# Ahead of the last mixer of a 1-core Trainium2 kernel: later constants, norm pieces of two tiles, rotation by transfers, later side steps

## The chip, the cores and the metric

One Trainium2 chip, one of its NeuronCores. The engines are named as the profile names them: PE (TensorE), DVE (VectorE), ACT (ScalarE), POOL (GpSimd) and SP (SyncE, which here only issues transfers). The metric is the device time of one execution in microseconds, and the median of several.

## What is computed

256 tokens with 2048 features pass through two blocks of two layers each. The first block:

```python
cos, sin = rope_tables(positions)
for layer in range(DEPTH):                       # DEPTH = 2
    if layer < N_A_LAYERS:
        mix = short_conv_mixer(x, a_w_in[layer], a_conv_w[layer], a_w_out[layer])
    else:
        k_sh, v_sh = shared_kv(x, kv_w_k, kv_w_v, cos, sin)
        mix = diff_attention(x, k_sh, v_sh, cos, sin, b_w_q[j], b_lambda[j],
                             b_subln_g[j], b_w_o[j], lambda_init)
    x = layer_norm(DEEPNORM_ALPHA * x + mix, ln_g[layer, 0], ln_b[layer, 0])
    ffn = conv_ffn(x, ffn_w_up[layer], ffn_conv_w[layer], ffn_conv_b[layer], ffn_w_down[layer])
    x = layer_norm(DEEPNORM_ALPHA * x + ffn, ln_g[layer, 1], ln_b[layer, 1])
```

The second block runs, on rmsnorm(h), a layer AB (dilated attention with three strides beside chunked gated linear attention, GLA), then a layer CD (an S5 state space mixer beside an HGRN mixer), each added to h, and ends with an rmsnorm:

```python
h = h + ab_layer(rmsnorm(h, norm_g[0]), ab_w_in, gla_w_gate, gla_b_gate, gla_norm_g, ab_w_out)
h = h + cd_layer(rmsnorm(h, norm_g[1]), cd_w_in, ..., hgrn_norm_g, cd_w_out)
return rmsnorm(h, final_g)
```

Two pieces of it are touched by name. The rotation of keys and queries works on the first 32 of each head's 128 features:

```python
x1, x2 = rot[..., :half], rot[..., half:]        # half = 16
rotated = concatenate([x1 * c - x2 * s, x2 * c + x1 * s], axis=-1)
```

and the attention's lambda is exp(sum(lam0·lam1)) − exp(sum(lam2·lam3)) + lambda_init.

## The kernel before

**Tiling.** Features lie on the partitions: XA[128, 16, 256] holds the residual stream in fp32 as 16 tiles of 128 features by 256 tokens, XH and XL the high and low bf16 halves of the activation that feeds the next product. A weight matrix is cut into chunks of 512 rows by 512 columns. Each product of fp32 numbers is three bf16 products (high·high, high·low, low·high), so that a chunk is 4 tiles × 4 column blocks × 3 = 48 matmuls of 128x256, about 5.2 us of PE.

**The road of a chunk.** SP loads it (1 MB) into the ring WF, three deep (L467). ACT casts it to the high half WH (L1169), DVE subtracts for the low half WL (L1746), both in a ring of five, up to LA = 3 chunks ahead of PE. PE multiplies in `gemm` (L652 on; all matmuls are recorded at L645, in the helper `mm`). The last KEPT = 46 chunks take another road: POOL loads them early in two pieces of 512 KB (L543), splits them (L552, L557) and stores both halves to DRAM (L554, L559), and SP loads halves at the end of the program (L460). `keep_begin(n)` says after which chunk of PE piece n is split.

**What sets the order.** Each engine runs a program of its own, written in the order in which it issues; nothing is scheduled. Work beside the products ("side flows") is written as generators, and a step of them (the code up to the next `yield`) is taken `rate` times per chunk: on PE after the second tile of a chunk and at its end, on ACT and DVE in one batch behind the split of the chunk three ahead. `idle(n)` is n empty steps. So one `yield` more puts the rest of a side flow later on that engine, by half a chunk of PE at rate 3. Engines wait in order: an instruction that waits holds up all behind it.

**Stages on PE** (us of the trace): short-conv mixer 0 to 251, its output product to 360, norm 0, feed-forward 364 to 1072, norm 1, keys and queries in eight groups of four chunks 1077 to 1262, values to 1375, output product to 1460, norm 2, feed-forward 1482 to 2183, norm 3, layer AB 2190 to 2640, layer CD 2640 to 3128, last rmsnorm to 3143.

**Places the change touches.**

- The start of SP's program: the order of the first loads (L474 to L490). CN are constants (identity, the rotation matrix `rope`, masks), PR the parameters, POSI the token positions.
- The layer norm: the norm is taken in pieces of the 16 tiles, EAGER = (first tile, tiles). DVE subtracts the mean (L1875) and multiplies by 1/sigma (L1894); ACT applies gain and bias in place (L1264 and L1270 for the first two tiles, L1275), copies the high half (L1279; at norm 3 it multiplies by the rmsnorm's gain, L1285); DVE makes the low half (L1859, at norm 3 L1854). PE takes the tiles in order as they become ready (the `ready` branch, L698 to L709).
- `attention_tables` and `lambda_sums`: angles and sines of the rotation on DVE and ACT, and lambda: two products on DVE (L2043, L2044), a column sum on PE, an exponential on ACT.
- The rotation: PE multiplies the first 32 rows of a key or query group by the 32x32 matrix `rope`, which swaps the two halves of 16 rows and changes a sign (the function `rotate`, four fp32 records each); DVE multiplies this by the sines (L2070), the rows themselves by the cosines (L2071), and adds (L2073).
- `diff_scores`, `heads`, `outputs`: scores, exponentials, the transposition ("turn"), products with the values and the norm of each head (L1328, L1331 on ACT, L2122, L2125 on DVE; OF is the tile of one head's output).
- Layer AB: `rms_sums`, `gla_decay` (DVE scan ahead of L1746), and the dilated heads: scores, softmax over three strides (L2300, L2301 on DVE end it), turn (L857 to L859 on PE), product.
- The end: DVE multiplies three groups of four tiles (L2531), POOL one (L636), SP stores four groups (L496).

Of the kernel before, what the change touches and what calls it, by code (L numbers as in the profile page):

```python
# [12 lines left out]
ALU = mybir.AluOpType  # L13
# [4 lines left out]
T = 256  # L18
# [9 lines left out]
FIRST = 4  # L28
KEPT = 46
# [17 lines left out]
CONST, NCONST = columns([("ident", 128), ("rope", 32), ("freq", 1), ("eps5", 1), ("eps6", 1), ("one", 1),  # L47
# [8 lines left out]
def constants():  # L56
# [7 lines left out]
    rope = np.zeros((128, 32))  # L64
    for i in range(16):
        rope[i + 16, i] = -1.0
        rope[i, i + 16] = 1.0
    put("rope", rope)
# [129 lines left out]
def two_block_model(nc, A, out):  # L198
    ctx = ExitStack()
    with ctx:  # L200
# [3 lines left out]
        def sem(name):  # L204
# [17 lines left out]
        ROOT = sb("ROOT", [128, 5])  # L222
        PSG = [ctx.enter_context(nc.psum_tensor(f"PSG{i}", [128, 4, T], F32)) for i in range(2)]
# [3 lines left out]
        d_in, d_pos, d_s5c, d_gw, d_cwst, d_csst, d_cwld = (  # L227
            sem(n) for n in ("d_in", "d_pos", "d_s5c", "d_gw", "d_cwst", "d_csst", "d_cwld"))
# [9 lines left out]
        d_out = [sem(f"d_out{i}") for i in range(2)]  # L238
# [15 lines left out]
        s_msq, s_var, s_sqrt, s_nrm, s_pre = (sem(n) for n in ("s_msq", "s_var", "s_sqrt", "s_nrm", "s_pre"))  # L254

        s_ang, s_trig, s_lamp, s_lams, s_lame = (sem(n) for n in ("s_ang", "s_trig", "s_lamp", "s_lams", "s_lame"))
        s_rot, s_rope, s_score, s_ss, s_max, s_exp, s_aa, s_tr, s_at = (
            sem(n) for n in ("s_rot", "s_rope", "s_score", "s_ss", "s_max", "s_exp", "s_aa", "s_tr", "s_at"))
# [15 lines left out]
        s_xw, s_rr, s_store, s_store_g = sem("s_xw"), sem("s_rr"), sem("s_store"), sem("s_store_g")  # L274
# [45 lines left out]

        def bcl(ap, n):
            return ap.unsqueeze(2).broadcast_to([ap.shape[0], ap.shape[1], n])
# [29 lines left out]
        EAGER = [(0, 1), (1, 1), (2, 2), (4, 4), (8, 4), (12, 4)]  # L352
# [45 lines left out]
        ATT = dict(SS=scr(13824, 2, 384), PP=scr(14592, 2, 384), SM=ASM, OF=scr(18816, 2, T), OQ=scr(19328, 2, T))  # L398
# [57 lines left out]
        def sync_program():  # L456
# [32 lines left out]
            for i in range(FIRST + 2, first_kept):  # L489
                load(i)  # L490
# [4 lines left out]
            def store(g, done_out):  # L495
                nc.sync.dma_start(out_v[:, 4 * g:4 * g + 4, :], four(XW, g)).then_inc(done_out, 16)  # L496
# [2102 lines left out]
```

## Time and profile before

| | |
|---|---|
| median of 3 runs | 3145.56 us |
| all runs | 3145.50, 3145.56, 3147.03 us |
| profiled execution | 3144.75 us |
| its span | 3143.4 us |
| mean granted clock of PE | 0.992 |
| PE busy | 3047.8 us (97%) |
| DVE, ACT, POOL busy | 2167.4 (69%), 1465.1 (47%), 680.8 us (22%) |
| data moved | 693 MB, mean 221 GB/s |

The profiled execution took 1.35 us more than its span, the time around the first and the last instruction. Matmul records overlap their neighbours, so that one row of 0.27 us stands for some 0.11 us of PE's time. The busy shares are those of the whole; the sections below go by stretches. A row of a timeline gives start, duration, engine, line, operation, what is written and read, how many in a row, and in brackets the idle time ahead of it with what ended it. The column "clock" of the windows is the share of PE's full clock that was granted: 1.00 is 2.4 GHz, 0.50 is 1.2 GHz.

### The profile page before, as it was taken

The numbers are of one execution on the slowest core, as the hardware profiler recorded it, in microseconds if no ns is written. First come the engines' busy times: TensorE is split into PE (matmuls) and PEld (weight loads), VectorE is DVE, ScalarE is ACT, GpSimd is POOL, SyncE is SP. The second block draws the span as 40 slices with busy tenths as digits, with TensorE's granted clock in tenths as the row PEclk, the third lists the DMA queues.
The fourth block names the chain that finished last, engine by engine and source line by source line (L and its number), as shares of the span: only waits on it lengthen the run. The fifth ranks groups of instructions, "written<-read, shape, count | busy, mean of one in ns | idle before, by whom it ended". The sixth has DMA issues, their size and how long they took to land. (4 is left out here: it accounts for less than half of the span.)

```text
span 3143.4 us, 58119 instructions
## 1 busy us (share of the span) xinstructions
PE 3047.8 (97%) x26006; PEld 2593.7 (83%) x26006; DVE 2167.4 (69%) x2028; ACT 1465.1 (47%) x1418; POOL 680.8 (22%) x753
## 2 busy tenths in 40 slices
PE   8999899999999999999999999999999999999988
PEld 7888788888888888568888888888687878776877
DVE  6777777777757666556767877655776556896655
ACT  4333454545444444564555555434564444212543
POOL 3555144545455200000210000000130000012300
PEclk9999999999999999999999999999999999999999
DMA  9889488888898564544666656754455545554343
GB/s 334 284 311 320 161 283 306 297 299 306 303 325 284 191 206 162 174 159 150 233 230 223 231 206 218 262 201 137 160 175 178 175 172 189 200 211 177 133 150 108
DMA packets 306025, 693.29 MB, mean 221 GB/s; under 512 B 16480, under 2 KB 20704, under 8 KB 299760
## 3 DMA queue, kind: packets, MB, share of 16 engines
q1 hardware_dynamic: 270192, 564.22, 52.1%
q0 software_dynamic: 35584, 125.36, 11.0%
q8 instruction: 204, 3.34, 0.4%
q14 instruction: 45, 0.37, 0.0%
HBM read 625.56 MB, written 63.96 MB: 219 GB/s over the span
## 5 line engine op out<-in xcount | busy, mean ns | idle before, releaser
L645 PE MATMUL PSG<-XH,WS 128*128 128x256 bf16 x11296 | 1846.5, 274 | 24.9 <-DVE WS L1963 7.4
L1746 DVE TENSOR_TENSOR WS<-WF,WS 128x2048 bf16<-128x2048 f32 (+1 forms) x483 | 1190.3, 2486 | 590.9 <-ACT WS L1169 590.3
L645 PE MATMUL PSG<-XL,WS 128*128 128x256 bf16 x5648 | 1490.4, 274 | 1.8 <-DVE XL L1854 1.1
L645 PEld LDWEIGHTS PSG<-XH,WS 128*128 128x128 bf16 x11296 | 1107.6, 98 | 173.6 <-issue 27.2
L1169 ACT ACTIVATE WS<-WF 128x2048 bf16<-128x2048 f32 (+1 forms) x483 | 906.0, 1899 | 632.7 <-PE PSG L645 216.9
L645 PE MATMUL PSG<-SCR,WS 128*128 128x256 bf16 x6720 | 745.5, 273 | 3.6 <-DVE SCR L2315 3.6
L645 PEld LDWEIGHTS PSG<-SCR,WS 128*128 128x128 bf16 x6720 | 659.5, 98 | 86.2 <-issue 4.2
L645 PEld LDWEIGHTS PSG<-XL,WS 128*128 128x128 bf16 x5648 | 554.0, 98 | 71.9 <-DVE XL L1859 2.4
L557 POOL TENSOR_TENSOR SCR<-SCR 128x1024 bf16<-128x1024 f32 x92 | 239.9, 2607 | 5.6 <-DMA weight_halves<-SCR 4.0
L645 PE MATMUL PSG<-WS,XH 128*128 128x512 bf16 x640 | 190.1, 379 | 2.2 <-issue 2.2
L645 PE MATMUL PB<-SCR 128*128 128x128 f32 (+3 forms) x928 | 151.2, 326 | 24.2 <-issue 7.8
L645 PEld LDWEIGHTS PB<-SCR 128*128 128x128 f32 (+2 forms) x928 | 126.4, 191 | 44.5 <-issue 24.6
L2018 DVE SCALAR_TENSOR_TENSOR SCR<-PSG,PR,SCR 128x254 f32<-128x254 f32 (+1 forms) x352 | 142.4, 471 | 17.7 <-ACT SCR L1398 17.1
L543 POOL DMA_DIRECT2D SCR<-cd_w_in x80 | 58.0, 725 | 415.8 <-PE PSG L645 401.1
L645 PEld LDWEIGHTS PSG<-WS,XH 128*128 128x128 bf16 x640 | 62.6, 98 | 76.7 <-issue 4.8
L1398 ACT ACTIVATE SCR<-PSG,PR 128x256 f32<-128x256 f32 x176 | 84.8, 562 | 69.4 <-PE PSG L645 69.3
L645 PE MATMUL PSG<-WS,XL 128*128 128x512 bf16 x320 | 116.1, 379 | 0.0
L552 POOL CAST SCR<-SCR 128x1024 bf16<-128x1024 f32 x92 | 110.6, 1203 | 3.5 <-PE PSG L645 3.4
L571 POOL DMA_DIRECT2D SCR<-s_cT_re x1 | 0.5, 542 | 437.8 <-DVE XL L1859 437.8
L1190 ACT ACTIVATE SCR<-PSG 128x1024 f32<-128x1024 f32 x30 | 30.6, 1020 | 133.1 <-PE PSG L645 133.1
L587 POOL DMA_DIRECT2D s_rotation<-SCR x16 | 8.5, 532 | 381.3 <-ACT SCR L1500 381.3
L525 POOL TENSOR_TENSOR SCR<-SCR 128x128 f32<-128x128 f32 x84 | 40.4, 482 | 174.0 <-PE PB L645 112.9
(267 smaller groups left out, 1779.7 us busy)
## 6 DMA issues: line engine op xcount, KB each, us to landing
WF<-ffn_w_up SPq DMA_DIRECT2D x176, 1024.0 KB, 6.5
WF<-ffn_w_down SPq DMA_DIRECT2D x88, 1024.0 KB, 6.4
WF<-ab_w_in SPq DMA_DIRECT2D x56, 1024.0 KB, 5.2
weight_halves<-SCR POOLq DMA_DIRECT2D x184, 256.0 KB, 6.0
WS<-weight_halves SPq DMA_DIRECT2D x46, 1024.0 KB, 4.8
WF<-a_w_in SPq DMA_DIRECT2D x44, 1024.0 KB, 8.9
SCR<-cd_w_in POOLq DMA_DIRECT2D x80, 512.0 KB, 6.9
WF<-a_w_out SPq DMA_DIRECT2D x16, 1024.0 KB, 8.0
```

The lines of the kernel that those rows point to most:

```text
L525: nc.gpsimd.tensor_tensor(to[:, :, 0:half], mid, src[:, :, 0:half], ALU.subtract)
L543: nc.gpsimd.dma_start(KW[n % 2], src).then_inc(d_keep[n % 2], 16)
L552: t = own.mark(nc.gpsimd.tensor_copy(KH, w))
L557: t = own.mark(nc.gpsimd.tensor_tensor(KL, w, KH, ALU.subtract))
L571: nc.gpsimd.dma_start(CT[i].rearrange("p a b -> p (a b)"), A[name]).then_inc(d_s5c, 16)
L587: nc.gpsimd.dma_start(CSD[n], TCS).then_inc(d_csst, 16)
L645: return nc.tensor.matmul(o, lhsT, rhs, start=start, stop=stop, skip_group_check=True)
L1169: act(shaped(WH, i % RB, rows, g["width"]), shaped(WF, r % RF, rows, g["width"]), ACT.Copy).then_inc(s_hi, 1)
L1190: act(dst, rowwise(ps) if row_major else ps[:, :, :], func, scale=scale).then_inc(s_evac[gi % 2], 1)
L1398: t = act(dst[:, n, :], ps[:, n, :], ACT.Identity, bias=pr("f_bias", 88 * l + f), scale=pr("f_conv", 264 * l + 176 + f))
L1746: tt(l, w, h, ALU.subtract).then_inc(s_lo, 1)
L2018: ins = stt(dst[:, n, sh:T], ps[:, n, 0:T - sh], pr("f_conv", 264 * l + 88 * tap + f), dst[:, n, sh:T], ALU.mult, ALU.add)
```

## The change

1. **Start.** CN and the positions are loaded behind the 32nd chunk, CN with a semaphore of its own; POOL's early pieces begin at chunk 10 and 12 of PE rather than 2 and 4, in the same total time; two chunks fewer are split early (KEPT 44).
2. **Norm.** EAGER has (4, 2), (6, 2) in place of (4, 4). For pieces of one or two tiles, and for all of norm 3, ACT makes the high half straight from XA with gain and bias as its scale and offset, and brings XA itself up to date after that. For norm 3 the gains are products made in advance (GWB). DVE's order is written anew (`multiply`, `whole`, `low`).
3. **PE within a piece:** the products with XH of all its tiles come first, then those with XL (`held`).
4. **Rotation.** The swap of the two halves of 16 rows is made by two DMAs of POOL (64 KB each) into the tile RT; the sign goes into the frequencies; PE's matmuls for it are gone. DVE waits for the DMAs (`d_swap`), PE's scores for the rotation (`s_rope`).
5. **Side steps.** `lambda_sums`, `diff_scores`, `heads`, `rms_sums`, `gla_decay` and the dilated heads have more empty steps; a second OF tile.
6. **End.** DVE multiplies all four groups, the last one in two halves; five stores instead of four.

The core of the diff:

```diff
-KEPT = 46
+KEPT = 44
+CONSTANTS_AT = 32
...
-    col[0:16, 0] = freq
+    col[0:16, 0] = -freq
     col[16:32, 0] = freq
...
-        EAGER = [(0, 1), (1, 1), (2, 2), (4, 4), (8, 4), (12, 4)]
+        EAGER = [(0, 1), (1, 1), (2, 2), (4, 2), (6, 2), (8, 4), (12, 4)]
...
-            nc.sync.dma_start(CN[:, :], A["consts"]).then_inc(d_in, 16)
             nc.sync.dma_start(PR[:, :], A["params"]).then_inc(d_in, 16)
+            for i in range(FIRST + 2, CONSTANTS_AT):
+                load(i)
+            nc.sync.dma_start(CN[:, :], A["consts"]).then_inc(d_cn, 16)
             nc.sync.dma_start(POSI, A["positions"].partition_broadcast(128)).then_inc(d_pos, 16)
...
-                return 4 + 2 * n if n < 28 else 67 + 2 * (n - 28)
+                return 12 + 2 * n if n < 24 else 67 + 2 * (n - 24)
...
-            nc.gpsimd.wait_ge(s_mm, 2)
+            nc.gpsimd.wait_ge(s_mm, 10)
...
+            for j in range(4):
+                for r, t in ((0, KA[j % 2]), (1, QA[j % 2])):
+                    nc.gpsimd.wait_ge(*evac(stage["kq"][2 * j + r]))
+                    if j or r:
+                        nc.gpsimd.wait_ge(s_rope, 2 * j + r)
+                    nc.gpsimd.dma_start(RT[16:32, :, :], t[0:16, :, :]).then_inc(d_swap, 16)
+                    nc.gpsimd.dma_start(RT[0:16, :, :], t[16:32, :, :]).then_inc(d_swap, 16)
...
-            nc.gpsimd.tensor_tensor(four(XW, 1), four(XW, 1), bc(STAT[:, 3, :], 4), ALU.mult).then_inc(s_store_g, 1)
...
-                            if ready[k] != seen:
-                                seen = ready[k]
-                                nc.tensor.wait_ge(*seen)
-                            for o, first, ab in sums:
-                                last = mm(o, *ab[1], False, sp)
+                            held += [(o, ab[1], sp) for o, _, ab in sums]
+                            if i < FIRST or kk == nk - 1 or ready[k + 1] != ready[k]:
+                                if ready[k] != seen:
+                                    seen = ready[k]
+                                    nc.tensor.wait_ge(*seen)
+                                for o, ab, stop in held:
+                                    last = mm(o, *ab, False, stop)
+                                held = []
...
             def lambda_sums():
-                yield
-                yield
-                yield
+                yield from idle(7)
                 nc.tensor.wait_ge(s_lamp, 1)
...
             def diff_scores(h, q, k, first):
+                nc.tensor.wait_ge(s_rope, 2 * (h // 2) + 2)
                 yield from scores(h, q, k, (first, first + 1))
-                yield
-                yield
+                yield from idle(3)
                 yield from turn(h, AA, (s_aa, h + 1))
...
-            def heads(j, gen):
-                yield from gen
-                yield
+            def heads(j):
+                yield from idle(4)
...
                     yield from scores(8 + h // 2, QD0, KD0, (h, h + 1))
+                    yield
                     yield
                     for c in range(2):
                         yield
...
                 for p, (a, n) in enumerate(EAGER):
                     nc.scalar.wait_ge(s_nrm, PIECES * L + p + 1)
+                    if L == 3 or n < 4:
+                        for k in range(a, a + n):
+                            w, b = high_affine(L, k)
+                            t = act(XH[:, k, :], XA[:, k, :], ACT.Identity, bias=b, scale=w)
+                        t.then_inc(s_xh, 1)
+                        if p >= 2:
+                            affine(a, n).then_inc(s_aff, 1)
+                        if p == 4:
+                            nc.scalar.wait_ge(s_pre, 2 * L + 2)
+                            nc.scalar.wait_ge(a_own, own.mark(affine(0, 2)))
                     else:
-                        weighted_high(0, a, n)
+                        affine(a, n).then_inc(s_aff, 1)
+                        nc.scalar.wait_ge(s_aff, (PIECES - 2) * L + p - 1)
+                        act(XH[:, a:a + n, :], XA[:, a:a + n, :], ACT.Copy).then_inc(s_xh, 1)
...
+                    OF = ATT["OF"][h % 2]
+                    yield from head_norm(h, 2, "eps5", OF, ATT["OQ"], h + 1, (s_nlo, h - 1) if h >= 2 else None)
...
             def rotate(n, dst):
                 yield
-                nc.vector.wait_ge(s_rot, n + 1)
+                yield
+                nc.vector.wait_ge(d_swap, 32 * (n + 1))
                 nc.vector.wait_ge(s_trig, 1)
...
-                tt(RT[0:32, :, :], sw, b32(SIN), ALU.mult)
+                tt(RT[0:32, :, :], RT[0:32, :, :], b32(SIN), ALU.mult)
...
                 t.then_inc(s_gabs, 1)
+                yield
+                yield
                 nc.vector.wait_ge(s_lg, 1)
...
-            for g in (0, 2, 3):
+            for g in range(4):
                 nc.vector.wait_ge(s_xw, g + 1)
-                tt(four(XW, g), four(XW, g), bc(rr, 4), ALU.mult).then_inc(s_store, 1)
+                for h in range(2 if g == 3 else 1):
+                    x = XW[:, 14:16, :] if h else XW[:, 12:14, :] if g == 3 else four(XW, g)
+                    tt(x, x, bc(rr, 2 if g == 3 else 4), ALU.mult).then_inc(s_store, 1)
```

How the instructions stand at three places (xN: a row repeated; in brackets the semaphores waited for).

**SP at the start, before.** WF is the weight ring, XA the input tiles.

```order
L472 DMA WF<-a_w_in 128x512 [waits s_lo0] x4
L467 DMA WF<-a_w_in 128x4x512 [waits s_lo0] x2
L486 DMA CN<-consts 128x2598
L487 DMA PR<-params 128x1082
L488 DMA SCR<-positions 128x256
L467 DMA WF<-a_w_in 128x4x512 [waits s_lo0]
L467 DMA WF<-a_w_in 128x4x512 [waits s_lo] x41
L467 DMA WF<-a_w_out 128x4x512 [waits s_lo] x16
```

Now:

```order
L475 DMA WF<-a_w_in 128x512 [waits s_lo0] x4
L470 DMA WF<-a_w_in 128x4x512 [waits s_lo0] x2
L489 DMA PR<-params 128x1082
L470 DMA WF<-a_w_in 128x4x512 [waits s_lo0]
L470 DMA WF<-a_w_in 128x4x512 [waits s_lo] x25
L492 DMA CN<-consts 128x2566
L493 DMA SCR<-positions 128x256
L470 DMA WF<-a_w_in 128x4x512 [waits s_lo] x16
```

CN and the positions stand behind 26 more chunk loads; the parameters stay.

**ACT at norm 0, before.** XH is the high half, XA the stream.

```order
L1264 ACTIVATE XH<-XA,PR 128x256 [waits s_nrm] x2
L1270 ACTIVATE XA<-XA,PR 128x256 [waits s_pre]
L1270 ACTIVATE XA<-XA,PR 128x256
L1275 ACTIVATE XA<-XA,PR 128x256 [waits s_nrm,a_own]
L1275 ACTIVATE XA<-XA,PR 128x256
L1279 ACTIVATE XH<-XA 128x512 [waits a_own]
L1275 ACTIVATE XA<-XA,PR 128x256 [waits s_nrm]
L1275 ACTIVATE XA<-XA,PR 128x256 x3
L1279 ACTIVATE XH<-XA 128x1024 [waits a_own]
L1275 ACTIVATE XA<-XA,PR 128x256 [waits s_nrm]
```

Now:

```order
L1261 ACTIVATE XH<-XA,PR 128x256 [waits s_nrm] x3
L1261 ACTIVATE XH<-XA,PR 128x256
L1252 ACTIVATE XA<-XA,PR 128x256 x2
L1261 ACTIVATE XH<-XA,PR 128x256 [waits s_nrm]
L1261 ACTIVATE XH<-XA,PR 128x256
L1252 ACTIVATE XA<-XA,PR 128x256 x2
L1261 ACTIVATE XH<-XA,PR 128x256 [waits s_nrm]
L1261 ACTIVATE XH<-XA,PR 128x256
L1252 ACTIVATE XA<-XA,PR 128x256 x2
L1252 ACTIVATE XA<-XA,PR 128x256 [waits s_pre]
L1252 ACTIVATE XA<-XA,PR 128x256
L1252 ACTIVATE XA<-XA,PR 128x256 [waits s_nrm,a_own]
```

The high halves of six tiles more are direct, ahead of the update of XA; tiles 4 to 7 are no longer one copy.

**PE at the first rotation, before.** PSG is the bank of the running product, PB the side bank, SCR the key tile, CN the constants.

```order
L645 MATMUL PSG<-XH,WS 128x256 x2
L645 MATMUL PSG<-XL,WS 128x256
L645 MATMUL PSG<-XH,WS 128x256
L645 MATMUL PB<-SCR,CN 32x512 [waits s_evac0]
L645 MATMUL PB<-SCR,CN 32x512
L645 MATMUL PSG<-XH,WS 128x256
L645 MATMUL PSG<-XL,WS 128x256
```

**POOL there, now.** SCR is both RT and the key and query tiles.

```order
L550 DMA weight_halves<-SCR 128x1024 [waits g_own]
L553 TENSOR_TENSOR SCR<-SCR 128x1024 [waits d_kl]
L555 DMA weight_halves<-SCR 128x1024 [waits g_own]
L570 DMA SCR<-SCR 16x1024 [waits s_evac0]
L571 DMA SCR<-SCR 16x1024
L570 DMA SCR<-SCR 16x1024 [waits s_rope,s_evac1]
L571 DMA SCR<-SCR 16x1024
```

PE's rows with CN at the rotation are gone; POOL's transfers, two for each of the eight groups, follow its last early split.

## Rows read from the trace of the kernel before

**Rows 1.** Page, part 1: busy time, share and instructions of PE.

```profile
PE 3047.8 (97%) x26006; PEld 2593.7 (83%) x26006; DVE 2167.4 (69%) x2028; ACT 1465.1 (47%) x1418; POOL 680.8 (22%) x753
```

**Rows 2.** PE's waits over the span: who waited, for whom, total us, times, longest.

```profile
PE PSG L645 <- ACT XH L1279: 6.8, 6, 1.5
...
PE PSG L645 <- DVE WS L1746: 5.5, 3, 4.3
...
PE PB L857 <- DVE SCR L2301: 5.4, 3, 3.3
PE PB L645 <- DVE SCR L2044: 5.2, 1, 5.2
PE PB L645 <- ACT SCR L1331: 4.8, 2, 3.2
...
PE PSG L645 <- issue: 2.2, 1, 2.2
PE PSG L645 <- ACT XH L1285: 2.1, 3, 1.2
...
PE PSG L645 <- DVE XL L1854: 1.1, 2, 0.6
```

**Rows 3.** Windows around 395 us: us, PE busy (records), clock, DMA share, GB/s.

```profile
394.10:397.50 3.40, 3.27 (x16) 0.50 0.67 197
397.50:402.50 5.00, 5.00 (x48) 1.00 0.83 286
```

**Rows 4.** Timeline, ACT, 38 to 41 us: start, us, operation, idle before it, releaser.

```profile
39.36 1.91 ACT L1169 ACTIVATE WS<-WF 128x2048 bf16<-128x2048 f32 x1 [8.26 <-DMA WF<-a_w_in]
```

**Rows 5.** Windows at the start, columns as in rows 3.

```profile
40.00:45.00 5.00, 0.71 (x7) 0.75 1.03 383
45.00:50.00 5.00, 5.00 (x28) 0.57 0.84 283
```

**Rows 6.** DMA issues: queue, count, KB each, median us from issue to landing.

```profile
CN<-consts SPq DMA_DIRECT2D x1, 1299.0 KB, 11.3
...
SCR<-s_bT_im POOLq DMA_DIRECT2D x8, 64.0 KB, 3.0
...
SCR<-positions SPq DMA_DIRECT2D x1, 128.0 KB, 12.1
```

**Rows 7.** Norm 0: timeline of ACT; line L1279 (ns min/median/max); timelines of PE, DVE.

```profile
376.25 2.08 ACT L1275 ACTIVATE XA<-XA,PR 128x256 f32<-128x256 f32 x4 [0.63 <-DVE XA L1894]
...
L1279 ACT ACTIVATE XH<-XA x12: 629/1057/1057, 368.2 to 1496.2; 128x1024 bf16<-128x1024 f32 x9, 128x512 bf16<-128x512 f32 x3
...
383.60 1.05 PE L645 MATMUL PSG<-XH,WS 128*128 128x256 bf16 x8
...
381.25 4.49 DVE L1746 TENSOR_TENSOR WS<-WF,WS 128x2048 bf16<-128x2048 f32 x2 [0.58 <-ACT WS L1169]
```

**Rows 8.** Rotation: PE by form over the span; then ACT, DVE, PE near 1130 us.

```profile
L645 PE MATMUL PB<-SCR,CN 32*32 32x512 f32 x32 | 15.2, 593 | 0.0
...
1125.14 1.02 ACT L1190 ACTIVATE SCR<-PSG 128x1024 f32<-128x1024 f32 x1 [8.02 <-PE PSG L645]
...
1130.20 1.21 DVE L2070 TENSOR_TENSOR SCR<-PB,SCR 32x1024 f32<-32x1024 f32 x1
...
1134.74 1.47 PE L645 MATMUL PB<-SCR 128*128 128x256 f32 x8
```

**Rows 9.** POOL's store issues at L554: duration ns min/median/max, first, last.

```profile
L554 POOL DMA_DIRECT2D weight_halves<-SCR x92: 540/557/575, 32.4 to 1055.2; - x92
```

**Rows 10.** Window at the first rotation, columns as in rows 3.

```profile
1100.00:1110.00 10.00, 10.00 (x80) 1.00 0.99 333
```

**Rows 11.** Timeline, ACT, 1390 to 1395 us.

```profile
1392.59 0.60 ACT L1328 ACTIVATE SCR<-PB 128x512 f32<-128x512 f32 x1 [0.82 <-DVE SCR L2125]
```

**Rows 12.** The end: line L2531 on DVE, and a window (DVE busy).

```profile
L2531 DVE TENSOR_TENSOR SCR<-SCR,STAT x3: 1210/1226/3362, 3132.8 to 3137.3; 128x1024 f32<-128x1024 f32 x3
...
3138.00:3143.40 5.40, 0.47 (x1) 0.50 0.85 291
```

More of the change, by code:

```diff
@@ L237, in two_block_model @@
         d_kh, d_kl = sem("d_kh"), sem("d_kl")
-        d_out = [sem(f"d_out{i}") for i in range(2)]
+        d_out = sem("d_out")
+        d_swap = sem("d_swap")
         d_bt = [sem(f"d_bt{i}") for i in range(2)]
@@ L913, in tensor_program @@
                     side.until(pairs[j - 2])
-                side.add(rotate(2 * j, KA[j % 2], gk))
+                side.add(idle(3))
                 gemm(gq, xh, xl, rate=3)
-                pairs.append(side.add(heads(j, rotate(2 * j + 1, QA[j % 2], gq))))
+                pairs.append(side.add(heads(j)))
             for j, gi in enumerate(stage["v"]):
@@ L924, in rms_sums @@
             def rms_sums():
-                yield from idle(7)
+                yield from idle(8)
                 sum_features(24, 1, True, False)
@@ L1304, in rms_first @@
                         yield
-                yield from idle(7)
+                yield from idle(9)
                 nc.scalar.wait_ge(s_sumrd, 28)
                 rms_root(0)
-                yield from idle(6)
+                yield from idle(4)
                 for p in range(4):
@@ L1420, in attention_tables @@
                 act(COS, TRT[:, 2, :], ACT.Sin, bias=cn("halfpi"), scale=-1.0).then_inc(s_trig, 1)
-                yield
-                yield
+                yield from idle(6)
                 nc.scalar.wait_ge(s_lams, 1)
@@ L1436, in diff_scores @@
                 exps(h, ATT["SS"], ATT["PP"], ASM)
-                yield
-                yield
-                yield
+                yield from idle(4)
                 nc.scalar.wait_ge(s_tr, h + 1)
@@ L1444, in heads @@
             def heads(j):
-                yield from idle(3)
+                yield from idle(4)
                 yield from diff_scores(2 * j)
@@ L1931, in rms_first @@
                         yield
-                yield from idle(8)
+                yield from idle(9)
                 rms_factor(0)
-                yield from idle(5)
+                yield from idle(4)
                 for p in range(4):
@@ L2044, in attention_tables @@
                 tt(ASM[:, 37:38], lb[:, 2:3], lb[:, 3:4], ALU.mult).then_inc(s_lamp, 1)
-                yield
-                yield
+                yield from idle(8)
                 nc.vector.wait_ge(s_lame, 1)
@@ L2107, in diff_scores @@
                 t.then_inc(s_aa, 1)
-                yield from idle(4)
+                yield from idle(5)
             def heads(j):
```

139 lines of the change are left out of this document (58 added, 81 removed).

## The prediction

> **What bounds the kernel now.** I read the page's busy shares first, then the list of what TensorE (PE) waited for, then the stretches around each wait. PE is busy for 3047.8 of 3143.4 us [rows 1], so a step shortens the program only if PE issues less in it, waits less, or runs at its full clock instead of half. The list of PE's waits [rows 2] gives the places that the diff touches: 5.5 us on DVE's weight halves (three waits, one of 4.3), 6.8 us in six waits on L1279 (the layer norms), 5.2 us in one wait on L2044 (lambda), 4.8 us in two waits on L1331 (the head norm; 3.2, and so 1.6), 5.4 us in three waits on L2301 (the dilated heads; the longest 3.3), 2.2 us in one "issue" gap, and 2.1 and 1.1 us in small ones at the fourth norm (L1285, L1854). A full stretch holds 48 matmuls in 5.00 us, about a chunk. A stretch of 3.40 us behind the lambda wait ran at 0.50 of the clock [rows 3]: it lost 1.7 us. I look for such a stretch behind each long wait, because it goes with the wait.
>
> **Start: −6.6.** ACT's split of a chunk at 39.36 us had waited 8.26 us for the weight transfer [rows 4]; PE, who gets the halves after ACT and DVE, stood 4.3 us [rows 2]. The windows show the transfer engines at 1.03 of their share, and then PE at 28 matmuls instead of 48 in 5 us, clock 0.57 [rows 5]: 20/48 of 5 us, with the bit ahead of 45 us 2.3 us. In this queue stand CN (1299 KB) and the positions, 11.3 and 12.1 us from issue to landing [rows 6], and POOL's early pieces beside them. What had to be moved ahead of that chunk's end is the chunk (1.05 MB), CN (1.33), the parameters (0.55), the positions (0.13) and POOL's two pieces (1.05), 4.1 MB; the change leaves 1.6. At the 383 GB/s of [rows 5] that is 6.5 us less; the chunk lands near 33.4 us (I take 6 us), its two splits (1.9 and 2.3 us) end near 37.7, ahead of 40.4, where PE asked. So 4.3 + 2.3. Low end 2, if other transfers fill the space. At the new place of the moved loads PE has hardly a wait on halves (1.2 us of [rows 2] in the rest of the program): 0. If that cover is gone it is CN's 1.3 MB at 383 GB/s, 3.4 us.
>
> **Lambda: −6.8.** PE waits 5.2 us for two tiny DVE products, which stand behind a table computation and a weight half. Four more steps on PE are two chunks at this rate, some 10 us, well behind the 5.2. The half-clock stretch of [rows 3] starts with this wait: 5.2 + 1.6. Low end 5.2, if the clock falls anyhow. What is late next are the halves, which stay in their order on DVE.
>
> **Norms 0 to 2: +1.8.** Here I don't take the 6.8 us as a gain. At the fourth chunk PE resumed at 383.60, when the halves that DVE began at 381.25 were done (two in 4.49, the first 2.29 long) [rows 7]: PE was bound there by the halves, which stand on ACT behind its whole norm chain, and what it had waited before was hidden in that. So ACT's chain decides. It gains six direct operations of 0.52 (four take 2.08) and loses two copies (0.63 and 1.06) [rows 7]: +1.4 us, of which its idle time (0.63 in [rows 7], two shorter ones ahead) takes a part. I take +0.6 for each of three norms; between 0 and +1.4 each. In the list one wait of some 2 us on DVE's halves takes the place of the second one on L1279.
>
> **Rotation: −15.2.** 32 records of the 32x512 fp32 matmul are 15.2 us of PE time [rows 8], with PE full around them. This goes for sure; what may come back is a wait for the swaps. POOL issues two DMAs of 64 KB, 0.56 us each, as L554 [rows 9]; 64 KB landed in 3.0 us [rows 6]. In the second group ACT's copy of the bank ran from 1125.14 to 1126.16, so the swap is in at 1126.2+0.6+0.6+3.0 = 1130.4; DVE's rotation, three operations of 1.21 us, began at 1130.20 before and so ended near 1133.8, and PE's scores came at 1134.74 [rows 8]; the program puts them now two chunks (10.5 us) behind the group's end, 1135.6. Margin 1.8. Price 0; between 0 and the late swaps below. The first swap falls where the transfer engines are at 0.99 [rows 10].
>
> **Attention outputs: −4.1.** Both waits on L1331 are for an ACT copy behind DVE's L2125, for which ACT stood 0.82 us [rows 11], since there was one OF tile. With two tiles and a step more the wait of 1.6 goes; of the 3.2 the 0.8 goes, and then it is under 3 us, so that I take off its half-clock stretch too, 1.7. (The 2.2 us gap had none behind it.) Ends: −2.4 and −6.5.
>
> **Norm 3: −0.7.** Its small waits (2.1 and 1.1) vanish with a half-clock stretch of 1.7, but PE then waits for the sums of the next norm, which DVE makes behind ACT's chain; these 4.9 us come back there, and +1.4 with them, since ACT's chain is that much longer. The issue gap of 2.2 us was DVE in gla_decay with the next half queued behind it; two more yields put the half first: −2.1. Ends −3 and +4, the upper one if the merged wait (7 to 8 us) is followed by twice that half-clock stretch.
>
> **Dilated heads: −5.2.** Of the three waits on L2301 the longest is 3.3, the others 0.8 and 1.3. A yield more moves each turn half a chunk (2.6 us): 0.8 gone, 3.3 to 0.7 with its half-clock stretch (1.7), 1.3 gone, but the last pair's turn and product now meet ahead of the output projection: +1.2. −0.8−2.6−1.7−1.3+1.2. Ends −2 and −7.
>
> **End: −2.0.** The middle DVE multiply took 3.36 us beside POOL's, the others 1.21 and 1.23 [rows 12]. Four at 1.22, the last in two halves of 0.69, end near 3137.9. The three stores behind the first moved for 0.85 of the last 5.4 us [rows 12], 1.53 us each; back to back, from 3134.7 (an estimate: 0.6 behind the first multiply), all four take 6.1 us and end near 3140.8; with the 0.3 us that I leave to the span's end, −2.3, less a fifth store's overhead. −0.7 to −2.4.
>
> KEPT 46 to 44 puts two more splits on ACT and DVE near 3015 to 3026, where PE waits for other things: 0, at most +2. The rest of the S5 and HGRN part stays.
>
> **Sum.** −6.6−6.8+1.8−15.2−4.1−0.7−5.2−2.0 = −38.8. The profiled execution took 3144.75 (span 3143.4), so 3105.95; the median of the runs shown is 0.8 us higher, so 3106.8, say 3107.
>
> **A rule that speaks against it.** 92 issues from POOL beside a busy DVE took 540 to 575 ns, and POOL's 64 KB loads landed in 3.0 us [rows 6, 9]: nothing held them. The Trainium skill, "SBUF — State Buffer", section "SBUF: two separate sides", says that GpSimd itself writes the descriptors of the DMAs it issues, and that it is shut out from that while DVE runs an operation in a two-port mode; it advises SP's or ACT's queue. By that rule the swaps would be late wherever DVE runs such an operation; the sum would stay −38.8 if that is never the case, and come to rival 1 if it is once or twice.
>
> **Rivals.** (1) One or two swaps land late, as the positions did under full transfer engines, 12.1 us [rows 6]. The rope is then 12.1−3.0−2.0 = 7.1 us too late for PE, with up to 3.4 us of half clock: +10.5, 3117. For: 0.99 in the first stretch [rows 10]. Against: it lasts 10 us, and the first scores come a group later. 0.12. (2) The norms: the merged chain costs 1.4 at each of three, norm 3 comes to +4, and gaps near 3 us draw half-clock stretches of 1.7 at three: (4.2−1.8)+4.7+5.1 = +12, 3119. For: PE then meets all its waits in one place. Against: the 2.2 us gap. 0.13. (3) The change doesn't do what it says at the start, since POOL's pieces and the weights still fill the queue: +4.6 to +6.6, 3113. 0.07. (4) The slower side: swaps queue behind the 1 MB weight loads in all four pairs. One late swap costs 10.5; four cost 42, and 4.6 more if the second transfer waits behind the first (its issue twice): 3107+42 = 3149, or 3154. It decides from a landing of about 12 us on; the 3.0 of [rows 6] is against it, the 12.1 for it. 0.03 for 3149, 0.03 for 3154.
>
> **How the numbers follow.** My forecast has 0.62 (3100 to 3112), the rivals 0.12, 0.13, 0.07 and 0.06. 0.2% (6.3 us) is about what a measurement of this kernel can tell from no change. Faster by more: 0.62+0.12+0.13+0.07 = 0.94; within 0.2%: 0.03; slower: 0.03. The range: the low ends (norms 0, outputs −6.5, norm 3 −3, dilated −7, end −2.4, the others as they stand) give −47.5, 3098; the high end takes in rivals 1 to 3, 3121.
>
> **What would show it.** PE's busy time falls by some 20 (15.2, and the half-clock stretches, four or five fewer) and its idle time by some 17. No wait of PE at 40 us, none at 389; at the fourth chunk of norms 0 to 2 a wait on DVE's halves near 2 us; no wait of PE's scores on the DVE rotation; five stores without a pause. It is wrong if swaps land after more than 5 us, or if waits of 3 us and more appear where small ones stood.

## The result, and the profile after

The changed kernel took 3114.08 us in the median of four runs (3113.43 to 3115.98), against 3146.30 us for the kernel before on the same chip (four runs, 3145.50 to 3147.96). The ratio is 0.9898, with an interval of 0.9887 to 0.9910: 32 us faster, forecast 39 (3107, range 3098 to 3121). The profiled execution of the changed kernel is the slowest of its four: 3115.98 us, span 3114.7, so the two profiles stand only 28.7 us apart, and the account by stages below adds up to that, but for rounding.

The page's busy shares after the change, to be held against [rows 1]:

```profile
PE 3028.3 (97%) x25950; PEld 2592.8 (83%) x25974; DVE 2163.2 (69%) x2047; ACT 1474.2 (47%) x1432; POOL 666.5 (21%) x748
```

PE is busy for 19.5 us less: 15.2 of it are the matmuls that are gone. The rest is not the clock. Ahead of the end, the trace before has nine stretches at half clock, 40.8 us in all, with PE busy for 35.0 of them; the trace after has eight, 44.2 us, with PE busy for 35.0 again. (24 matmul records of the values' product are missing from the trace after, 25950 beside 25974 weight loads; what else makes up the rest is open.) With 28.7 us less of span PE's idle time falls by only 9. Its list of waits (who waited for whom, total us, times, longest), to be held against [rows 2]:

```profile
PE PB L645 <- DVE SUMS L1756: 10.4, 6, 6.4
PE PSG L645 <- DVE WS L1736: 9.4, 7, 2.1
...
PE PSG L645 <- DVE XL L2320: 4.8, 1, 4.8
PE PSG L645 <- ACT XH L1271: 3.9, 3, 1.3
...
PE PB L645 <- ACT SCR L1322: 2.3, 1, 2.3
PE PB L645 <- ACT SCR L1180: 1.5, 1, 1.5
...
PE PB L847 <- DVE SCR L2306: 1.0, 1, 1.0
```

The wait on lambda's products (5.2) is gone, that on the dilated turn fell from 5.4 to 1.0, the head norm's from 4.8 to 2.3, the "issue" gap of 2.2 is gone. Others grew: the weight halves from 5.5 to 9.4 (now L1736, seven times, none longer than 2.2), the wait for the sums to 10.4 with one of 6.4 that was not there, and the last one of the dilated stage (L2320, 2.9 before) to 4.8.

By stage (all numbers us, negative where the changed kernel is faster):

| stage | forecast | measured |
|---|---|---|
| start, to the first norm's sums | −6.6 | −5.6 |
| lambda | −6.8 | −3.1 |
| norms 0 to 2 | +1.8 | −0.1 |
| rotation | −15.2 | −15.5 |
| attention outputs | −4.1 | −2.3 |
| norm 3 and gla_decay | −0.7 | +1.2 |
| dilated heads | −5.2 | −2.6 |
| S5 and HGRN | 0 | +0.9 |
| end | −2.0 | −1.7 |
| sum | −38.8 | −28.8 |

The first row and the last four are read off from one of PE's waits to the next in both traces. The rows from lambda to the attention outputs lie between PE's resuming behind the first norm's sums and its resuming behind the head norm's wait (338.48 to 1393.73 us before, 332.88 to 1367.16 after), 21.0 us less. They are split by PE's weight loads for the main products: there are 24,624 of them in every trace here, in the same order, so that the time between the same two loads can be compared. From the load that stands at 386 us before to the one at 420 us (lambda and the first chunks of the feed-forward), PE took 34.0 us before and 31.0 after.

**Start.** The windows of the start (us, PE busy and records, clock, transfer share, GB/s), for [rows 5]:

```profile
30.00:35.00 5.00, 4.24 (x40) 1.00 0.67 217
35.00:40.00 5.00, 5.00 (x49) 1.00 0.88 297
40.00:45.00 5.00, 5.00 (x49) 1.00 0.79 262
```

No wait and no half clock at 40 us (one wait of 0.76 us stands at 30.9), and the transfer engines no longer at 1.03. In the twelve profiled runs below, which all keep both loads late or one of them, PE reached the first norm's sums at 329.2 to 330.6 us, and here at 331.1 (336.6 before), so the −5.6 of this trace is −6.0 to −7.4 in the others.

**Norm 0** has now a wait for the high halves and then the one on the weight halves (DVE) that the prediction looked for, 1.69 us. **Rotation.** DVE's operation with its wait, and the landing times of POOL's two transfers of each swap (min, median, max):

```profile
1100.39 1.21 DVE L2071 TENSOR_TENSOR SCR<-SCR 32x1024 f32<-32x1024 f32 x1 [0.41 <-DMA SCR<-SCR]
...
DMA to landing us min/median/max: 2.1/2.5/4.2
...
DMA to landing us min/median/max: 2.2/3.5/4.3
```

The longest swap took 4.3 us; DVE waited 2.9 us for four of the eight, PE for none.

**Norm 3.** ACT's last pieces and first weight split, PE's wait for the sums, and the window that holds its end and the half clock behind it. This one wait stands where [rows 2] had the small ones on L1285 and L1854:

```profile
2178.08 2.06 ACT L1252 ACTIVATE XA<-XA,PR 128x256 f32<-128x256 f32 x4
2180.17 1.91 ACT L1159 ACTIVATE WS<-WF 128x2048 bf16<-128x2048 f32 x1
...
2186.26 1.22 PE L645 MATMUL PB<-SUMS,ONE_D 128*128 128x256 f32 x2 [6.37 <-DVE SUMS L1756]
...
2183.10:2193.30 10.20, 6.43 (x24) 0.50 0.33 104
```

**End.** Five multiplies in 4.70 us, the stores back to back at 0.93, for [rows 12]:

```profile
3105.84 4.70 DVE L2538 TENSOR_TENSOR SCR<-SCR,STAT 128x1024 f32<-128x1024 f32 x5
...
3105.00:3108.00 3.00, 0.00 (x0) 0.50 0.00 0
3108.00:3114.70 6.70, 0.00 (x0) 0.50 0.93 313
```

### The profile page after: what moved, and what is told of

Same layout as the page of the kernel before. It is cut to its first block and busy times, and to the rows that moved or that the text cites. A ratio compares the mean times of both kernels' runs of the same rounds, so it can differ in the third digit from the quotient of the medians.

```text
span 3114.7 us, 58088 instructions
## 1 busy us (share of the span) xinstructions
PE 3028.3 (97%) x25950; PEld 2592.8 (83%) x25974; DVE 2163.2 (69%) x2047; ACT 1474.2 (47%) x1432; POOL 666.5 (21%) x748
## 5 line engine op out<-in xcount | busy, mean ns | idle before, releaser
L1736 DVE TENSOR_TENSOR WS<-WF,WS 128x2048 bf16<-128x2048 f32 (+1 forms) x485 | 1189.3, 2475 | 563.9 <-ACT WS L1159 563.5
L553 POOL TENSOR_TENSOR SCR<-SCR 128x1024 bf16<-128x1024 f32 x88 | 221.8, 2521 | 4.5 <-DMA weight_halves<-SCR 3.1
L645 PE MATMUL PSG<-WS,XH 128*128 128x512 bf16 x621 | 180.9, 379 | 0.7
L1401 ACT ACTIVATE SCR<-SCR 128x1024 bf16<-128x1024 f32 x22 | 23.3, 1057 | 99.3 <-DVE SCR L2030 99.3
```

The costliest lines, as they stand in the source:

```text
L553: t = own.mark(nc.gpsimd.tensor_tensor(KL, w, KH, ALU.subtract))
L645: return nc.tensor.matmul(o, lhsT, rhs, start=start, stop=stop, skip_group_check=True)
L1401: act(four(HH, j), HF, ACT.Copy).then_inc(s_hh, 1)
L1736: tt(l, w, h, ALU.subtract).then_inc(s_lo, 1)
```

## The experiments

All are the changed kernel with one edit more, beside the kernel before (3145.9 to 3147.0 in these sessions). Medians of four runs.

### e1 and e5: POOL's splits kept away from lambda's place

```diff
# e1
-                return 12 + 2 * n if n < 24 else 67 + 2 * (n - 24)
+                return 12 + 2 * n if n < 25 else 73 + 2 * (n - 25)
# e5
-                return 12 + 2 * n if n < 24 else 67 + 2 * (n - 24)
+                return 12 + 2 * n if n < 24 else 73 + 5 * (n - 24) // 3 if n < 42 else 67 + 2 * (n - 24)
```

Why this question: in the changed kernel lambda's wait is gone and PE waits a little later. DVE's half, POOL's split beside it, PE's wait, and the window behind it:

```profile
389.05 3.80 DVE L1736 TENSOR_TENSOR WS<-WF,WS 128x2048 bf16<-128x2048 f32 x1 [0.79 <-ACT WS L1159]
...
389.64 1.05 POOL L548 CAST SCR<-SCR 128x1024 bf16<-128x1024 f32 x1
...
391.56 3.27 POOL L553 TENSOR_TENSOR SCR<-SCR 128x1024 bf16<-128x1024 f32 x1
...
401.24 0.28 PE L645 MATMUL PSG<-XH,WS 128*128 128x256 bf16 x1 [2.15 <-DVE WS L1736]
...
401.40:404.80 3.40, 3.40 (x18) 0.50 0.81 243
```

> The changed kernel with POOL's early splits kept out of chunks 67 to 72 (one more piece at chunk 60, the next at 73, 75 and so on). In the changed kernel PE waits 2.15 us at 399 us on DVE's halves and a half-clock stretch (1.7 us) follows; a DVE half at 389.05 took 3.80 us beside a POOL split where one takes 2.29 us. Theory 1 (POOL's piece makes the half late, and the wait that the lambda step left uncovered it): wait and stretch vanish, 3114.1 - 3.9 = 3110.2 us. Rival (the halves of the first feed-forward chunks are late by DVE's and ACT's own work, whatever POOL does): the wait stays at about 2 us, 3114 us.

3116.64 us: slower, not faster. At 399 us the wait and the half-clock stretch are gone, as theory 1 said, but the pieces hit two other places. POOL's split at chunk 60 falls on the weight half ahead of the sums of norm 0 (4.28 us in place of 2.29), and the last ones, now up to chunk 197, on norm 1. Between the same weight loads PE took 4.0 us less at lambda than in the changed kernel, but 3.0 more at norm 0 and 2.6 more at norm 1. DVE and POOL at norm 1, and PE's wait for the first sums (1.82 in the changed kernel):

```profile
1072.97 2.06 DVE L1881 TENSOR_TENSOR XA<-XA,STAT 128x1024 f32<-128x1024 f32 x1
1075.06 3.04 DVE L1871 TENSOR_TENSOR XA<-XA,STAT 128x1024 f32<-128x1024 f32 x1
...
1072.41 1.53 POOL L548 CAST SCR<-SCR 128x1024 bf16<-128x1024 f32 x1 [12.83 <-PE PSG L645]
...
1074.80 2.22 POOL L553 TENSOR_TENSOR SCR<-SCR 128x1024 bf16<-128x1024 f32 x1
...
333.89 0.83 PE L645 MATMUL PB<-SUMS,ONE_D 128*128 128x256 f32 x2 [3.80 <-DVE SUMS L1756]
```

Two DVE operations that take 1.22 us elsewhere took 2.06 and 3.04. POOL's cast ended at 1073.94 and DVE's first at 1075.03, 1.1 later; POOL's subtraction ended at 1077.02 and DVE's second at 1078.10, 1.1 later. Both ran for their own time only from the end of POOL's operation on. The Trainium skill, "SBUF — State Buffer", section "SBUF: two separate sides", describes this: a DVE operation with two SBUF inputs and a GpSimd operation that reads SBUF lock each other out for the whole instruction. The trace agrees, within 0.15 us.

Which of the two gives way is not always so plain: the half of 389.05 us in the changed kernel began 0.6 us ahead of POOL's cast, and still it was the half that took longer.

The whole trace of the changed kernel shows the same. Of DVE's 484 weight halves of 128x2048, the 360 that ran apart from POOL's casts and subtractions took 2.27 to 2.51 us; the 124 beside them took 3.05 in the median and up to 4.44. The ten operations of 128x1024 with an input in PSUM that ran beside POOL's took 1.22 to 1.23 us, as they do alone.

> As e1, but without a piece at chunk 60 and with the last pieces where they were: POOL leaves out chunks 67 to 72 and catches up between chunks 73 and 103 (five chunks for three pieces). Theory 1 (a POOL split beside DVE's work lengthens DVE's operations; it costs where PE waits for DVE): the wait of 2.15 us at 399 us and the half-clock stretch behind it vanish as in e1, and e1's new waits at 330 us (3.80 in place of 1.82) and at 1080 us (2.05) don't appear: 3114.1 - 3.9 = 3110.2 us. Rival (what e1 took away comes back wherever POOL's work goes): 3113 to 3116 us.

3109.66 us, −4.4 against the changed kernel (theory 1: −3.9). The same DVE half, and PE's waits on halves:

```profile
384.79 2.29 DVE L1736 TENSOR_TENSOR WS<-WF,WS 128x2048 bf16<-128x2048 f32 x1 [0.79 <-ACT WS L1159]
...
PE PSG L645 <- DVE WS L1736: 6.8, 6, 1.8
```

3.80 us became 2.29, and the wait of 2.15 us is gone. The rival falls. From the load at 386 us before to the one at 420, PE took 27.0 us here, against 31.0 in the changed kernel and 34.0 before: 7.0 us of gain, where 6.8 were forecast. So what ate the gain at lambda was DVE beside POOL.

### e2: lambda's steps as before

```diff
             def lambda_sums():
-                yield from idle(7)
+                yield from idle(3)
```
(and 6 to 2 on ACT, 8 to 2 on DVE)

> The changed kernel with the old number of empty steps before lambda's sum and exponential (3, 2, 2 in place of 7, 6, 8). Theory 1: the wait of 5.2 us on the two lambda products comes back with its half-clock stretch (1.6), and it covers the wait of 2.15 us at 399 us and its stretch again: 3114.1 + 6.8 - 3.9 = 3117.0 us. Rival (the two are independent): 3114.1 + 6.8 = 3120.9 us.

3116.90 us, +2.8 (theory 3117.0). The wait is back, and no wait stands at 399 us:

```profile
387.14 0.58 PE L645 MATMUL PB<-SCR,ONE 128*128 128x2 f32 x2 [4.94 <-DVE SCR L2048]
```

Undoing the step costs 2.8 us, not 6.8: the old wait covers the later one. Between the two loads at lambda PE took 34.9 us, 4.0 more than in the changed kernel; 1.7 of that came back because the later wait of 2.30 us near 1368 us had no half-clock stretch in this trace.

### e3 and e4: the start, each half undone

```diff
# e3
-CONSTANTS_AT = 32
+CONSTANTS_AT = 6
# e4
-                return 12 + 2 * n if n < 24 else 67 + 2 * (n - 24)
+                return 4 + 2 * n if n < 24 else 67 + 2 * (n - 24)
-            nc.gpsimd.wait_ge(s_mm, 10)
+            nc.gpsimd.wait_ge(s_mm, 2)
```

> The changed kernel with the constants (1283 KB) and the positions loaded behind chunk 5 again, POOL's pieces late as in the change. If the 1.43 MB of constants were what held the chunk at 39 us, PE's wait near 40 us comes back for the most part (3 to 4 us and a half-clock stretch of 2.3): 3118 to 3120 us. If POOL's pieces were, next to nothing: 3114 to 3115 us. By bytes (1.4 MB against 1.05 MB of POOL's loads and as much of its stores) I expect the constants to hold the larger part, a wait of about 1 to 2 us: 3116 us.

3114.67 us, within a microsecond of the change, and I had expected 3116. The windows at the start, and then the wait at 399 us with the window behind it:

```profile
35.00:40.00 5.00, 5.00 (x49) 1.00 0.74 272
40.00:45.00 5.00, 5.00 (x49) 1.00 0.93 302
...
399.41 0.28 PE L645 MATMUL PSG<-XH,WS 128*128 128x256 bf16 x1 [2.15 <-DVE WS L1736]
...
399.50:402.90 3.40, 3.40 (x32) 1.00 0.67 208
```

> The changed kernel with POOL's pieces from chunk 2 and 4 on again, the constants late as in the change. If POOL's loads and stores were what filled the queue at 39 us, PE's wait comes back: 3118 to 3120 us. If the constants were, 3114 us. With e3 this splits the 6.6 us of the start; if both come out near 3114 us, only the two together fill the queue.

3114.38 us, the same. The windows at the start:

```profile
35.00:40.00 5.00, 5.00 (x49) 1.00 1.06 398
40.00:45.00 5.00, 5.00 (x48) 1.00 0.96 321
```

In neither is there a wait at 40 us (e4 has one of 1.28 us at 30.5, where the changed kernel has 0.76). Each of the two moves alone takes the whole wait of 4.3 us away; only both loads together make the chunk late. The second move brought nothing more that these runs can tell. In e3's trace the stretch at half clock that is missing at 399 us is not all gain: a wait of 1.92 us on a weight half follows at 422.6 us, which the changed kernel doesn't have.

### e6, e7, e8: the norms

```diff
# e6: EAGER and both layer_norm functions as before
-        EAGER = [(0, 1), (1, 1), (2, 2), (4, 2), (6, 2), (8, 4), (12, 4)]
+        EAGER = [(0, 1), (1, 1), (2, 2), (4, 4), (8, 4), (12, 4)]
# e7
-                            if i < FIRST or kk == nk - 1 or ready[k + 1] != ready[k]:
+                            if True:
# e8, in ACT's layer_norm
+                    if L == 3 and p >= 2:
+                        affine(a, n).then_inc(s_aff, 1)
+                        nc.scalar.wait_ge(s_aff, (PIECES - 2) * L + p - 1)
+                        weighted_high(0, a, n)
```

> The changed kernel with the old norm: pieces (1, 1, 2, 4, 4, 4), gain and bias in place before the copy or the weighted copy, at all four norms; the order of PE within a piece stays new. Theory 1 (at norms 0 to 2 PE is bound by the halves behind ACT's chain in either form, at norm 3 the longer chain costs 1.4 us and a longer half-clock stretch): 0 at norms 0 to 2, -3 at norm 3, 3111 us. Rival (the pieces of two tiles save PE's waits of 0.76 us at three norms and more at the fourth): 3114.1 + 2.3 + 1 = 3117 us.

3112.56 us, −1.5.

> The changed kernel with PE's old order within a piece: per tile the products with XH, then those with XL. Theory 1 (PE's end of each norm is set by ACT's chain and the halves, so the order inside only moves the waits): 3114 us, with small waits on XL at norm 3 again and the wait for the sums shorter by as much. Rival (the order saves PE 0.2 to 0.5 us at each norm): 3115 to 3116 us.

3113.86 us, no difference (theory 1): at norm 3 the wait for the sums is 3.7 us instead of 6.4, with 3.0 us of waits on the low halves in front of it.

> The changed kernel with norm 3 alone put back for tiles 2 to 15: gain and bias in place first, then the high half by the rmsnorm's gain (0.43 us a tile) rather than direct from XA (0.51 us). Theory 1 (ACT's chain sets when the sums of the next norm start): ACT ends 14 x 0.08 = 1.1 us sooner, PE's wait for the sums falls from 6.4 to about 5.3 us, 3113.0 us, and 3111.3 us if the half-clock stretch of 10.24 us behind it is one step shorter. Rival (PE then waits as much for the high halves, which come later in each piece): 3114 us.

3112.47 us, −1.6. PE's two waits:

```profile
2174.67 3.65 PE L645 MATMUL PSG<-XH,WS 128*128 128x256 bf16 x32 [1.48 <-ACT XH L1283]
...
2184.20 1.22 PE L645 MATMUL PB<-SUMS,ONE_D 128*128 128x256 f32 x2 [4.14 <-DVE SUMS L1763]
```

The wait for the sums fell to 4.14 us, with waits of 0.65 and 1.48 us on the high halves ahead of it (one of 0.42 in the changed kernel). PE resumed behind the sums 0.6 us sooner, counted from the sums of norm 2; the half-clock stretch behind it was 6.8 us instead of 10.2. In e11 and e12, which have the same edit, PE resumes by the same 0.6 us sooner, but the norm as a whole took 75.0 and 74.8 us between the same loads, as good as in the changed kernel (75.3), and not the 73.5 of e8. (In e6 PE resumed 0.8 us sooner, and the norm took 73.1.) So of the 1.6 us of e8 only 0.6 is shown to be the form of norm 3; the rest is time at half clock, which doesn't come each time.

Norms 0 to 2 differ by 0.1 us each between e6 and the changed kernel, and by less in e7: there old and new form are worth the same, and so is the order inside a piece. The rivals of e6 and e7 fall; that of e8 (the wait only moves to the high halves) is right for the larger part of the wait.

### e9 and e12: the dilated stage's end

```diff
                         yield from turn(8 + h + c, GLA["PP"][:, c, :], (s_aa, 8 + h // 2 + 1))
-                        yield
+                        if (h, c) != (4, 0):
+                            yield
```
(e12 does the same to one of the two steps behind that pair's first product)

> The changed kernel with one of PE's steps taken out again after the first turn of the third pair of dilated heads, so that the turn is half a chunk later as in the change, but the products and turns behind it stand where they stood before. In the changed kernel the waits ahead of the output projection grew from 4.9 us (1.32, 0.63, 2.91) to 7.5 us (1.44, 1.24, 4.79). Theory 1 (ACT, which waits 3.61 us for that pair's last product in both kernels, paces the chain that ends the stage; a product half a chunk later puts the chain 2.6 us later): the three waits fall to about 4.9 us, 3114.1 - 2.6 = 3111.5 us. Rival (the stage's end is paced by the last pair's own scores or by DVE's halves): the waits stay near 7.5 us, 3114 us.

3113.84 us; my theory fell. Counted from the wait ahead of that pair's turn, the product came 2.6 us sooner, and PE resumed only 0.5 us sooner. PE's last product of the third pair, the last pair's scores, and the resuming:

```profile
2506.02 0.82 PE L645 MATMUL PB<-SCR 128*128 128x256 f32 x4
...
2511.91 1.47 PE L645 MATMUL PB<-SCR 128*128 128x256 f32 x8
...
2533.28 0.37 PE L645 MATMUL PSG<-XH,WS 128*128 128x256 bf16 x1 [4.79 <-DVE XL L2321]
```

In the kernel before and in the changed one, PE's last scores and its resuming stand as far apart as they do here to within half a microsecond. Before:

```profile
2541.31 1.47 PE L645 MATMUL PB<-SCR 128*128 128x256 f32 x8
...
2563.16 0.37 PE L645 MATMUL PSG<-XH,WS 128*128 128x256 bf16 x1 [2.91 <-DVE XL L2315]
```

And after the change:

```profile
2513.41 1.47 PE L645 MATMUL PB<-SCR 128*128 128x256 f32 x8
...
2535.26 0.37 PE L645 MATMUL PSG<-XH,WS 128*128 128x256 bf16 x1 [4.79 <-DVE XL L2320]
```

21.85 us in both, 21.4 here. So the chain of DVE and ACT that ends the stage seems to start at the last pair's scores, and it is they that the additional steps had put half a chunk later (24 weight loads of the main product). e12 puts this to the test, on top of the edits of e11:

> e11 with one more step of PE taken out, behind the first product of the third pair of dilated heads: now the last pair's scores stand where they stood before (chunk 448.3 of PE's order; in the change and in e9 and e11 at 448.8), while the third pair's first turn stays half a chunk later. Theory, formed after e9 (in both kernels PE resumes 21.85 us behind the last pair's scores; those set the chain of DVE and ACT that ends the stage): the time from PE's end ahead of the third pair's turn to its resuming falls by 2.6 us against the change's 45.87, to about 43.2 us (e9: 45.4), and the whole to 3106.8 - 2.1 = 3104.7 us. Rival (the stage's end is paced by the halves or the products, not the scores): 45 us and 3106.8 us again.

```profile
2504.69 1.47 PE L645 MATMUL PB<-SCR 128*128 128x256 f32 x8
...
2526.54 0.37 PE L645 MATMUL PSG<-XH,WS 128*128 128x256 bf16 x1 [4.45 <-DVE XL L2329]
```

The stretch from the wait ahead of the third pair's turn (2483.29) to the resuming took 43.25 us, against 45.4 in e9 and 45.9 in the changed kernel, as forecast. The whole took 3106.54 us (3105.00 to 3108.36), where 3104.7 was expected: in the profiled run the 2.1 us were spent again on half clock that e11's did not have (behind the head norm's wait at 1359 us, near 2959 us, and 1.0 us more behind the stage's own last wait). So the 2.1 us are shown in the stage and not in the whole.

### e10: the rotation by PE again

```diff
-                tt(RT[0:32, :, :], RT[0:32, :, :], b32(SIN), ALU.mult)
+                tt(RT[0:32, :, :], sw, b32(SIN), ALU.mult)
```
(with `rotate` on PE, the matrix `rope`, and no swap transfers)

> The changed kernel with the rotation by PE's matmuls again (32 records, no swap transfers), all else as changed. Theory 1: PE gets back 15.2 us of work in full stretches and no wait goes away for it: 3114.1 + 15.2 = 3129.3 us. Rival (the swaps cost something of their own, such as DVE's waits of 0.4 to 1.2 us for four of them, or weight loads held up by 16 more transfers): 3126 to 3128 us.

3129.01 us, +14.9. PE's busy time, and the records of the rotation (its line is L642 in this kernel):

```profile
PE 3041.6 (97%) x26006; PEld 2593.1 (83%) x26006; DVE 2157.5 (69%) x2047; ACT 1473.4 (47%) x1432; POOL 659.2 (21%) x732
...
L642 PE MATMUL PB<-SCR,CN 32*32 32x512 f32 x32 | 15.2, 594 | 0.0
```

Between the same weight loads the rotation's stretch took 202.0 us before, 202.0 in e10 and 186.5 in the changed kernel: 15.5. Swaps by transfers cost nothing of their own.

### e11: e5, e8 and e9 together

```diff
-                return 12 + 2 * n if n < 24 else 67 + 2 * (n - 24)
+                return 12 + 2 * n if n < 24 else 73 + 5 * (n - 24) // 3 if n < 42 else 67 + 2 * (n - 24)
...
+                    if L == 3 and p >= 2:
...
+                        if (h, c) != (4, 0):
+                            yield
```

> The changed kernel with the edits of e5 (no POOL split in chunks 67 to 72), e8 (norm 3 with gain and bias in place first) and e9 together. They lie in different stages, so they should add: 3114.1 - 4.4 - 1.6 - 2.6 = 3105.5 us, up to 1.7 us off by a half-clock stretch more or less.

3106.83 us (3106.41 to 3108.28), 0.9879 of the kernel before (0.9864 to 0.9894), where 3105.5 was expected; e9 gave 0.5 and not 2.6 us of that, and e8's edit 0.6 and not 1.6. What made up for them are two stretches at half clock that the changed kernel has and e11's trace has not (behind the wait of 2.30 us at 1361.7 us and the one of 3.00 at 2959.7), some 1.7 us each; that the sum came near is in part luck. e11 and e12 are the fastest here, some 7 us under the changed kernel.

## Why the prediction was right, and where it was off

**Right.** The direction, the range (3098 to 3121) and the largest term. The measured 3114.1 lies outside the narrower 3100 to 3112 that the forecast itself had; it is near the 3113 of rival 3, but by chance, for the start did what the change says. The rotation's 15.2 us were the 32 records' busy time (e10: 14.9); the swaps landed in 2.5 to 3.5 us in the median, where the row of 64 KB said 3.0, and none took more than 4.3, so that neither rival 1 nor rival 4 came, and nothing was to be seen of the delay in the rule that spoke against it. The start gave 5.6 us here and 6.0 to 7.4 in the other traces for the 6.6 of the forecast, though not for the reason worked out: of "4.1 MB; the change leaves 1.6" either part would have been enough (e3, e4). The end gave 1.7 of 2.0. At the norms the step "I don't take the 6.8 us as a gain" held: the waits on L1279 went over to a wait on the halves; the +0.6 each, however, was −0.1 to 0, so ACT's extra 1.4 us didn't reach PE. At norm 3 the chain cost PE 1.0 us of the +1.4: it resumed behind the sums 25.6 us earlier, having been 26.5 ahead.

**Off: lambda, by 3.7 us.** The step that failed is "What is late next are the halves, which stay in their order on DVE". I named the next one and costed it at nothing. The half begun at 389 us took 1.5 us more than alone, beside POOL's split; the feed-forward's first convolution stands behind it on DVE, ACT waits for that, and PE waits for the next halves: 2.15 us and a half-clock stretch. The old wait had covered this (e2), and POOL was its cause (e5, and e1 at the same place).

**Off: the dilated heads, by 2.6 us.** "A yield more moves each turn half a chunk" is so, and the 3.3 fell to 1.04 us. But a step in a side flow moves all behind it too, the last pair's scores among it, which start a chain of 21.85 us (e9, e12). For the waits at the stage's end the forecast had −1.3 and +1.2, in sum nothing; those three waits went from 4.9 to 7.5 us, 2.6 more. This is also one of the prediction's own signs of being wrong, a wait of 4.8 us where one of 2.9 stood.

**Off: the half-clock stretches.** The forecast took off 2.3 us at the start, 1.6 at lambda, 1.7 at the outputs and 1.7 at the dilated heads, 7.3 in all, and PE's work at half clock came out the same as before, 35.0 us: in net none of it came, which is most of the 10 us by which the two sums differ. "PE's busy time falls by some 20" was reckoned with four or five such stretches fewer; the 19.5 agree with it by number only, and the idle time fell by 9 and not 17. Of the outputs' gap the prediction said "it is under 3 us, so that I take off its half-clock stretch too, 1.7"; its rows had one gap of 2.2 us without a stretch and none between that and 3.2. The gap of 2.29 us had one:

```profile
1367.16 1.89 PE L645 MATMUL PB<-SCR,ONE 128*128 128x256 f32 x4 [2.29 <-ACT SCR L1322]
...
1367.30:1370.70 3.40, 3.40 (x13) 0.51 0.55 214
```

The stretch is 1.7 of the 1.8 us by which the outputs missed: in the five traces without it this part took 3.9 us less than before, against the 4.1 of the forecast. At norm 3 the merged wait drew 10.2 us of half clock where 3.4 stood before, part of it with PE idle. It cost 2.3 us behind the sums; less the 0.4 by which the chain was shorter than forecast, that is the miss there. S5 and HGRN got 0.9 us longer, by a wait of 3.00 us that both kernels have. Before, with the window behind it:

```profile
2996.11 0.89 PE L645 MATMUL PB<-SCR 128*128 128x256 f32 x4 [3.00 <-issue]
...
2997.20:3000.60 3.40, 3.40 (x34) 1.00 0.02 7
```

After:

```profile
2967.05 0.89 PE L645 MATMUL PB<-SCR 128*128 128x256 f32 x4 [3.00 <-issue]
...
2968.20:2971.60 3.40, 3.40 (x19) 0.51 1.02 394
```

With what follows this cost 2.0 us, and 1.1 came back since PE was idle for more of the half clock at the end of the dilated stage.

The same wait is not always followed by such a stretch. Of eight profiled kernels with the wait of 2.13 to 2.15 us near 399 us, four had the stretch and four not (e3 above is one without); of thirteen with the one of 2.29 to 2.30 us behind the rotation (near 1363 us, 1381 in e10), eight; of all fourteen, nine had it behind the 3.00 us. What decides it is open. Each is worth some 1.7 us, as much as what e6 and e8 measured in the whole.

## What to carry to other kernels

A wait that is removed gives back only as much as the next resource is early: look up what stood idle during it, and what other engine's work (POOL's, here) falls beside it once the order in time has moved. A step added in a side flow moves everything behind it, so ask which operation starts the last chain of the stage. Work taken off a full engine counts in full when what replaces it fits into another engine's idle time.

## What the runs showed of the hardware

DVE operations with two inputs in SBUF stood still while POOL's cast or subtraction ran (in e1 1.22 us became 2.06 and 3.04, ending 1.1 us behind POOL's end both times; in the changed kernel a weight half took 3.80 in place of 2.29). DVE operations of 1.22 us with one input in PSUM took no longer beside them. Transfers from SBUF to SBUF of 64 KB issued by POOL landed in 2.1 to 4.3 us beside a DVE that was busy for 72% of that stretch (1095 to 1262 us), mostly with such operations; none was held up. The clock fell to half behind waits of 2.15 us in some traces and not in others, and behind one of 3.00 us likewise. A wait of 6.4 us drew 10.2 us of half clock in the changed kernel and 6.8 in e10; one of 4.1 us drew 6.8 in e8, e11 and e12.
